# Triangular inverses of the mixer: two VectorE transposes per level in place of copies and transposing products

## The reference

```python
def rwkv7_scan(r, w, k, v, kk, a, reverse):
    def step(state, inp):
        r_t, w_t, k_t, v_t, kk_t, a_t = inp
        sa = jnp.einsum('bhvk,bhk->bhv', state, -kk_t)
        state = (state * w_t[:, :, None, :] + sa[..., None] * (kk_t * a_t)[:, :, None, :]
                 + v_t[..., None] * k_t[:, :, None, :])
        return state, jnp.einsum('bhvk,bhk->bhv', state, r_t)
    _, ys = lax.scan(step, s0, xs, reverse=reverse)
```

## Time and profile before

| | |
|---|---|
| Median of 3 runs | 3039.8 us (3039.72 to 3046.81) |
| The profiled execution's own time | 3051.22 us |
| Its span | 3049.3 us |
| Mean granted TensorE clock, share of full | 0.982 |
| TensorE matmuls busy | 2695.5 us (88%) |
| VectorE busy | 2080.1 us (68%) |
| ScalarE busy | 1351.0 us (44%) |

### The profile page before, as it was taken

How to read it: one execution, slowest core, us unless ns; L and a number is a source line. 1 busy time by engine, 2 the same in 40 slices (tenths; PEclk the granted TensorE clock), 3 DMA queues, 4 the chain that set the end, 5 groups by cost and what they waited for, 6 DMA issues and landing times. The chain is left out here.

```text
span 3049.3 us, 45561 instructions
## 1 busy us (share of the span) xinstructions
PE 2695.5 (88%) x17032; PEld 1810.3 (59%) x17032; DVE 2080.1 (68%) x3862; ACT 1351.0 (44%) x3008; POOL 581.6 (19%) x516
## 2 busy tenths in 40 slices
PE   7999987999999998899989999877777999777777
PEld 6887775788788777678877655323222655322322
DVE  6765765786776576467745687777774786777764
ACT  5443445543444345444434344444443444444443
POOL 0000000000000000000000344444442344444442
PEclk9999999999999999899999999999999999999999
DMA  8855201696776520248761799999998999999997
GB/s 312 283 189 179 93 4 44 239 306 247 247 278 208 181 90 4 99 176 299 272 237 51 299 426 427 426 427 427 427 427 352 362 426 426 427 427 426 428 427 312
DMA packets 257166, 864.18 MB, mean 283 GB/s; under 512 B 15664, under 2 KB 139440, under 8 KB 184496
## 3 DMA queue, kind: packets, MB, share of 16 engines
q0 software_dynamic: 73728, 536.90, 41.9%
q1 hardware_dynamic: 183216, 324.36, 30.3%
HBM read 852.55 MB, written 8.65 MB: 282 GB/s over the span
## 5 line engine op out<-in xcount | busy, mean ns | idle before, releaser
L484 PE MATMUL banks<-weight_parts_hi,normedT_hi 128*128 128x512 f32 (+2 forms) x1152 | 453.8, 394 | 21.2 <-DVE weight_parts_lo L1447 8.7
L486 PE MATMUL banks<-weight_parts_hi,normedT_lo 128*128 128x512 f32 (+2 forms) x1152 | 441.9, 384 | 0.0
L485 PE MATMUL banks<-weight_parts_lo,normedT_hi 128*128 128x512 f32 (+2 forms) x1152 | 441.9, 384 | 0.0
L3956 PE MATMUL banks<-raw_weights,diagonals 128*128 128x512 f32 x744 | 351.8, 612 | 77.8 <-ACT diagonals L186 77.6
L3836 POOL DMA_INDIRECT constants<-peer_rows,expert_ids x48 | 54.8, 1142 | 1813.4 <-DVE expert_ids L153 1751.9
L3956 PE MATMUL banks<-query_weights,diagonals 128*128 128x512 f32 x640 | 308.0, 618 | 67.8 <-ACT diagonals L186 67.6
L186 ACT ACTIVATE gelu<-dots 128x1 f32<-128x1 f32 x512 | 102.1, 199 | 477.9 <-DVE dots L162 477.3
L3956 PEld LDWEIGHTS banks<-raw_weights,diagonals 128*128 128x128 f32 x744 | 136.0, 192 | 283.0 <-ACT diagonals L186 156.5
L162 DVE CUSTOM_DVE_ANT_0 modulation<-raw_weights,normed 128x1024 f32<-128x1024 f32 x186 | 228.1, 1226 | 105.6 <-DMA raw_weights<-peer_rows,expert_ids 94.7
L3956 PE MATMUL banks<-modulation,diagonals 128*128 128x512 f32 x472 | 226.9, 611 | 47.9 <-ACT diagonals L186 47.5
L3956 PEld LDWEIGHTS banks<-query_weights,diagonals 128*128 128x128 f32 x640 | 118.0, 194 | 249.4 <-ACT diagonals L186 142.1
(11 more groups left out here) (431 smaller groups left out, 4821.3 us busy)
## 6 DMA issues: line engine op xcount, KB each, us to landing
raw_weights<-ffn_in SPq DMA_DIRECT2D x86, 1024.0 KB, 7.6
side_weights<-mod_tiles SPq DMA_DIRECT2D x48, 1024.0 KB, 5.5
raw_weights<-ffn_out SPq DMA_DIRECT2D x44, 1024.0 KB, 6.4
raw_weights<-w_in SPq DMA_DIRECT2D x28, 1024.0 KB, 5.0
query_weights<-peer_w_q SPq DMA_DIRECT2D x16, 1024.0 KB, 10.6
raw_weights<-w_in SPq DMA_DIRECT2D x10, 1536.0 KB, 6.5
raw_weights<-w_branch SPq DMA_DIRECT2D x8, 1024.0 KB, 7.3
raw_weights<-w_out SPq DMA_DIRECT2D x8, 1024.0 KB, 5.8
```

What stands on the lines that cost most here:

```text
L484: nc.tensor.matmul(out, lhs.hi, rhs.hi, start=start, stop=False)
L485: nc.tensor.matmul(out, lhs.hi, rhs.lo, start=False, stop=False)
L486: return nc.tensor.matmul(out, lhs.lo, rhs.hi, start=False, stop=stop)
L3956: last = nc.tensor.matmul(k.bank(2 * j + half), diag[:, g % DIAGS, :], ring.rows(g)[:, D + half * BANK:D + (half + 1) * BANK], start=t == ...
```

## The change

The product gm' xT and ScalarE's copy of it are gone, and so are the bank that held xT and the extra products that prepared the untransposed start (L2038, L2049, L2068, L2095). VectorE now transposes the new X from its bank to xT, drains, and transposes xT back to x. Its transpose works on blocks of 32x32, and up to level 4 the inverse has no entries outside of such blocks. The masks of levels 1 to 5 now include the diagonal and I is added to A, so that the product xT' gm is the whole new X and VectorE's addition falls away. `across` and `by_turns` are gone: every product reads and writes the same chunk's partitions.

The side work moves as well. The multiplications for `ends` stand behind both lanes' scaling, those for `decay_diagonal` go to `beside`, between lane 0's transposes and lane 0's next mask. ScalarE's square root goes from the end of tile 0 to tile 1, behind the copies of the turned keys. The gate products of `dve_products` go to the end of each pass.

```diff
-            merge.append((cr // (2 * b) == cc // (2 * b)) & (cr // b != cc // b) & later)
+            merge.append((cr // (2 * b) == cc // (2 * b)) & (cr // b != cc // b) & later | (cr == cc) & (lv > 0))
...
-    across = {n: [chunks[(ch + n // NPAIR) % 2] for ch in range(2)] for n in range(NHA)}
-    by_turns = [e * NPAIR + q for q in range(NPAIR) for e in range(2)]
...
                     for n in LEVELS:
                         for g, (ex, m, mT, s1, ends, x, dw, wc, xT, gm, akv, xa, u0) in enumerate(lanes):
                             if n == 1:
 
                                 wait_act(g, j, "akv")
-                            wait_dve(g, j, f"x{n - 1}")
-                            for h in by_turns:
-                                for cs, to in zip(chunks, across[h]):
-                                    last = nc.tensor.matmul(k.bank(4 * g + 2 + h // NPAIR)[to, h % NPAIR * CH:h % NPAIR * CH + CH],
+                                wait_dve(g, j, "x0")
+                            else:
+                                wait_dve(g, j, f"t{n - 1}")
+                            for h in range(NHA):
+                                for cs in chunks:
+                                    last = nc.tensor.matmul(k.bank(4 * g + 2 + h // NPAIR)[cs, h % NPAIR * CH:h % NPAIR * CH + CH],
                                                             s1[cs, h, 0, :], x[cs, h, :], start=True, stop=True)
...
-                                for h in range(NHA):
-                                    for to in across[h]:
-                                        last = nc.tensor.matmul(k.bank(4 * g + 1)[to, cols[h]], gm[to, h, :], xT[to, h, :],
-                                                                start=False, stop=True, skip_group_check=True)
...
+                                    if n < LEVELS[-1]:
+                                        last = nc.tensor.matmul(k.bank(4 * g + 2 + h // NPAIR)[cs, at:at + CH], xT[cs, h, :],
+                                                                gm[cs, h, :], start=True, stop=True)
...
+                    if j:
+                        norm.act_roots(act, o)
...
-                            act.wait_ge(on_pe[g], ON_PE.count(j, f"t{n}"))
-                            if n < LEVELS[-1]:
-                                o.copy(xT, k.bank(4 * g + 1, NHA, CH), free=True).then_inc(on_act[g], 1)
...
+                        o.mul(xT, s1[:, :, 0, :], masks[1 - g])
+                        o.add(s1[:, :, 0, :], s1[:, :, 0, :], eye)
+                        o.add(xT, xT, eye, free=True)
+                        dve.drain()
+                        nc.vector.transpose(x[:, :, :].rearrange("p h n -> p (h n)"),
+                                            xT.rearrange("p h n -> p (h n)")).then_inc(on_dve[g], 1)
...
+                    for g in range(2):
                         merge(g, 1)
                     for n in LEVELS:
-                        for g in range(2):
-                            if n > 1:
-                                merge(g, n)
                         for g, (ex, m, mT, s1, ends, x, dw, wc, xT, gm, akv, xa, u0) in enumerate(lanes):
                             if n < LEVELS[-1]:
                                 wait_pe(g, j, f"x{n}")
-                                o.add(by_e(x), by_e(x), k.ps[:, 4 * g + 2:4 * g + 4, SEQ:].rearrange("p e (q n) -> p e q n", n=CH),
-                                      free=True).then_inc(on_dve[g], 1)
+                                nc.vector.transpose(xT.rearrange("p (e q) n -> p e (q n)", e=2),
+                                                    k.ps[:, 4 * g + 2:4 * g + 4, SEQ:])
+                                dve.drain()
+                                nc.vector.transpose(x[:, :, :].rearrange("p h n -> p (h n)"),
+                                                    xT.rearrange("p h n -> p (h n)")).then_inc(on_dve[g], 1)
...
+                            if g == 0:
+                                beside(n)
+                            if n < LEVELS[-1]:
+                                merge(g, n + 1)
+                    norm.dve_products(o, j, 0)
+                    norm.dve_products(o, j, 1)
```

More of the change, by code:

```diff
@@ L1863, in head, with act_squares @@
         return self.qk[:, j, n * HA:(n + 1) * HA]
-    def act_squares(self, act, o, level, g):
+    def act_squares(self, act, o, level):
         S = self.k.sem
-        if level == 1 and g == 1:
+        if level == 3:
             act.wait_ge(S["prod"], 1)
             o.fn(self.l2[:, :], self.l2[:, :], ACT.Exp, free=True).then_inc(S["lam_exped"], 1)
[L1871 to L1887, removed]
+        for i in range(*self.part(level - 1, 6)):
+            j, n = divmod(i, self.HEADS)
+            last = o.fn(self.junk[:, :], self.head(j, n), ACT.Square, total=self.ss[:, j, n:n + 1], free=i == 0)
+        if level == 6:
+            last.then_inc(S["squared"], 1)
+    def act_roots(self, act, o):
+        S = self.k.sem
+        act.wait_ge(S["reduced"], 1)
+        if self.other is not None:
+            o.fn(self.other[:, :, 0], self.other[:, :, 0], ACT.Sqrt, free=True)
+        o.fn(self.ss[:, :, :], self.ss[:, :, :], ACT.Sqrt, free=True).then_inc(S["rooted"], 1)
@@ L1896, in dve_small @@
         S = self.k.sem
-        if level == 1:
+        if level == 3:
             dve.wait_ge(S["loaded"], self.loaded)
@@ L1902, in dve_small @@
             o.ts(self.gain_col[:, :], self.gain_col[:, :], HA ** -0.5, ALU.mult)
-            o.sum(self.l2[:, :], self.products[:, :, :]).then_inc(S["prod"], 1)
-        if level == 2:
+            o.sum(self.l2[:, :], self.products[:, :, :], free=True).then_inc(S["prod"], 1)
+        if level == 4:
             dve.wait_ge(S["lam_exped"], 1)
@@ L2033, in _ @@
                     for g, (ex, m, mT, s1, ends, x, dw, wc, xT, gm, akv, xa, u0) in enumerate(lanes):
[L2035 to L2040, removed]
                         wait_dve(g, j, "score3")
@@ new lines, in _ @@
+                                wait_dve(g, j, f"t{n - 1}")
+                            for h in range(NHA):
+                                at = SEQ + h % NPAIR * CH
+                                for cs in chunks:
+                                    if n < LEVELS[-1]:
+                                        last = nc.tensor.matmul(k.bank(4 * g + 2 + h // NPAIR)[cs, at:at + CH], xT[cs, h, :],
+                                                                gm[cs, h, :], start=True, stop=True)
+                                    else:
+                                        last = nc.tensor.matmul(k.bank(4 * g + 1 + h // NPAIR * 2)[cs, cols[h % NPAIR]], gm[cs, h, :], xT[cs, h, :],
+                                                                start=True, stop=True)
```

133 lines of the change are left out of this document (56 added, 77 removed).

## The result

| | before | changed |
|---|---|---|
| Median | 3041.9 us (4 runs, 3039.7 to 3046.8) | 3074.4 us (4 runs, 3068.9 to 3079.9) |
| Ratio, 95% interval | | 1.0105 (1.0079 to 1.013) |
| The profiled execution's span | 3049.3 us | 3078.0 us |
| TensorE's mean granted clock | 0.982 | 0.971 |

A forecast was written before the change was run, and what follows sets the result against it. TensorE bounds the levels before, VectorE's order after. Inverses +18.6, tile 1's wait -2.8 and the softmax's load +1.3 sum to +17.1 us: 3057 us on the median of 3039.8, range 3044 to 3080.

The forecast's parts named there:

- The serial level: In the inverses, VectorE makes lane 1's transposes only after lane 0's mask: 6.87 us a level against 5.28, +18.6 us.
- The price of a transpose: VectorE's transposes in the levels: 0.69 us each, like every 128x512 operation out of a bank.
- The clock: TensorE's granted clock in the inverses: expected to stay at 1.00 despite sparser products.
- the prediction's own sign: Forecast is wrong if levels take under 5.5 us, transposes are far from 0.69, or granted clock leaves 1.00 inside passes.
- the rival: TensorE's clock falls in the levels: 15 us more if in half of them (3072), 3087 in all; chance 13%.
- Tile 1's wait: Lane 1's scaling in tile 1 no longer stands behind lane 0's `ends` and `decay_diagonal`: -2.8 us in two passes.
- The softmax's load: ScalarE must load the softmax's own table after the square root's: +1.3 us in layer 0, taken up in layer 1.
- Behind the levels: At a pass's end, gate products lie beside L2105 to L2124 and the first pause may go: counted as nothing.
- the forecast's own 3050 to 3064: The main forecast's own range, from pauses, side work and the profiled execution lying 11 us above the median; chance 62%.

The follow-up runs named there:

- the run with two corners: The kernel before, with every product of a level reading and writing the same chunk's partitions: 3054.2 us, ratio 1.0029 to before.
- the kernel that was kept busy: The changed kernel plus identity products nobody reads, ahead of level 1 and behind lane 0's G of each level: 3057.3 us, ratio 1.005 to before.

## Why the prediction was right or wrong

- **The serial level: right.** VectorE's order sets it. Another order, an earlier G, or one operation less ahead of G each took the loss away. The sum took the two-corner products as given; how much of the level's 7.04 us they are is open (see the run with two corners).
- **The price of a transpose: right.** 0.69 was taken; it is 0.70 to 0.72 out of a bank and 0.71 out of SBUF. The estimate that the prediction worked out from the Trainium skill's 311 ns for a bf16 transpose of 128x128 ("VectorE: DVE Perf Modes", the three transpose paths) was 0.71, and the trace agrees. The level came out at 7.04 instead of 6.87: G starts 0.02 to 0.04 us later behind the transposes than reckoned, lane 0's G is read after 1.20 us and not 1.15, and lane 0's X starts 0.99 behind lane 1's G and not 0.93. A pass at the full clock takes 37.2 us and not 36.5, some 3 us over four passes.
- **The clock: the step that failed.** The forecast kept it at 1.00 and gave its fall 13%, arguing with TensorE's share over a whole level (3.7 of 6.87 us) and with a sparse start that had stayed at 1.00. Both arguments fail. The share is an average: a level's products lie in one clump, and the 3.10 us ahead of the fall shown held 1.30 of TensorE's work. And the start had stayed at the full clock with the very products that the change takes out (L2038, L2049, L2068); without them it fell in all four passes. By the prediction's own sign (the granted clock leaves 1.00 inside the passes) the forecast was wrong here, and the rival came true. That the rival's price, 15 us for half of the levels, is near the 13.8 us that the unread products won back is in part luck: 5.5 of the 13.8 lie in the starts, which the rival did not count. The Trainium skill ("TensorE: Matmul & The Clock Gate", the HAM clock gate) calls half rate the default that activity lifts; the falls, and their absence where TensorE was kept busy, agree.
- **Tile 1's wait: right in size, half right in cause.** -2.8 was forecast, -2.9 measured. But the multiplications alone are 0.5 us a pass of it and the load alone nothing; that it needs both edits is argued, and no run shows it.
- **The softmax's load: wrong.** +1.3 us was forecast "in layer 0 that chain waits for nothing else". ScalarE in the changed kernel:

```profile
506.17 1.28 ACT L186 ACT_TABLE_LOAD   x1
511.14 0.47 ACT L186 ACTIVATE logits<-banks,row_max 128x256 f32<-128x256 f32 x1 [3.69 <-DVE row_max L153]
```

  The load is there, but ScalarE then still waits 3.69 us for VectorE's maximum. The idle time of 4.99 us ahead of that exponential stood in the earlier trace rows; it was room for the load, and was read only as "started by VectorE".
- **Behind the levels: counted as nothing, -4.0 us.** TensorE's waits from lane 1's last level copy to the copy of the state in the first pass (line waited at, what ended it, total us, times, longest), first of the kernel before, then of the changed one. "Issue" marks time in which the engine waited for nothing that the profile shows:

```profile
PE banks L2115 <- issue: 1.2, 1, 1.2
PE banks L2133 <- issue: 1.2, 2, 0.7
PE banks L2105 <- issue: 0.7, 1, 0.7
```

```profile
PE banks L2106 <- issue: 1.1, 2, 0.7
PE banks L2088 <- issue: 0.3, 1, 0.3
```

  Over the four passes these pauses sum to 11.9 and 7.6 us, which covers the 4.0. Why there are fewer no run shows. The prediction looked at the first pause alone. The gate products on VectorE held no product of TensorE back, as assumed: no wait behind the levels has another cause than "issue".
- **The total.** The forecast's mechanism without a fall of the clock is the kernel that was kept busy: 3057.3 us, where the forecast was 3057. That they agree so closely is luck: the inverses are 21.5 us longer and not 18.6, the softmax's 1.3 did not come, and the stretches behind the levels are 4.8 us shorter and not equal. The changed kernel itself, at 3074.4, is outside the forecast's own 3050 to 3064, by the clock. It is inside the range because the range reached up to the rival of the clock.

## What to carry to other kernels

Where two lanes share an engine that works in order, write down for each level which instruction waits with the other lane's work behind it: here the order, not the sum of the busy times, made 7.0 us of 5.4. Put only what the next product needs ahead of it (here a copy, which another engine can make), and the transpose beside the product. Where a change takes work from TensorE, do not take its share of a whole stretch as proof that the granted clock stays: here a fall that the forecast had left out cost 13.8 us, and a run with unread products in the pauses gave its price.

## What the runs showed that was not expected

- Products that nobody reads made a kernel faster: 17.1 us in the medians with 27 more a pass (13.8 of it in the inverses), and 9.7 us with 7 more (6.2).
- A table load of 1.28 us that visibly delays the next instruction moved the inverse behind it by nothing. The multiplications alone moved it by 0.5 us; the kernel before, with both, took 1.42 more.
- Slower products can cost less than their difference: in the kernel before 4 x 0.41 us more a level came to 0.4, since TensorE's pauses marked "issue" and its wait for the masks went away.
